# Large on-chip buffers start at multiples of 128 bytes in a decoder layer on one core

## The chip, the cores and the metric

One core of a Trainium2 chip runs the whole layer as one program. Its engines are TensorE (PE in the profile, its weight loads PEld), VectorE (DVE), ScalarE (ACT), GpSimd (POOL) and SyncE (SP), which issues all DMA transfers here. The metric is the device time in microseconds, the median of several executions. The change is about byte addresses within a partition of the on-chip memory (SBUF): every tensor has 128 rows, one for each partition, and starts at the same byte offset in all of them.

## What is computed

A decoder layer over 256 tokens of width 2048, in float32: an input projection, a diagonal state-space branch and a latent attention branch side by side, merged by gates, an output projection with a layer norm, and a gated feed-forward network with a second layer norm.

```python
z = h @ w_in[l]
u_ssm, c_q, c_kv, k_rope_raw, gate_logits = jnp.split(z, split_at, axis=-1)
y_ssm = s5_scan(u_ssm, ...)
glu_a, glu_b = jnp.split(jax.nn.gelu(y_ssm) @ w_glu[l], 2, axis=-1)
ssm_out = glu_a * jax.nn.sigmoid(glu_b)
q = (rms_norm(c_q, q_norm_g[l]) @ w_uq[l]).reshape(bsz, seq, N_HEADS, QK_NOPE + QK_ROPE)
kv = (rms_norm(c_kv, kv_norm_g[l]) @ w_ukv[l]).reshape(bsz, seq, N_HEADS, QK_NOPE + V_HEAD)
mla_out = mla_attention(q_nope, q_rope, k_nope, k_rope, v)
g_ssm, g_mla = jnp.split(jax.nn.sigmoid(gate_logits), 2, axis=-1)
mix = (g_ssm * ssm_out + g_mla * mla_out) @ w_out[l]
h = layer_norm(DEEPNORM_ALPHA * h + mix, ln1_g[l], ln1_b[l])
ffn = (jax.nn.silu(h @ w_ffn_gate[l]) * (h @ w_ffn_up[l])) @ w_ffn_down[l]
h = layer_norm(DEEPNORM_ALPHA * h + ffn, ln2_g[l], ln2_b[l])
```

The feed-forward width is 5632, so its three matrices are most of the weights.

## The kernel before

All weights are packed by the host into 454 slabs of 128 x 1024 float32 (512 KB, 4 KB for each partition) in the order of use. SyncE loads them one after the other into `raw`, a ring of four slots. For each slab ScalarE writes a rounded copy of the type fp32r to `whi` (`high`, L466), and VectorE writes the remainder raw - whi to `wlo` (`low_part`, L421; in the head stage GpSimd takes 16 of them). The activations are split in the same way into a high and a low half, side by side in one buffer. A product of float32 precision is then three fp32r products: high with high, high with low, low with high.

Three helpers on TensorE write these products out:

- `fold_tile` (L823 to L825): stationary operand is a 128 x 128 block of whi or wlo, moving operand 256 columns of the activations. Three matmuls of 256 columns. It runs in the projection stage and for the gates (activations `xT`), in the head stage for the latent projections (`cT`) and in the GLU stage (`yT`).
- `feature_tile` (L834, L837): the same stationary operand; one matmul has the high and the low half, 512 contiguous columns, as its moving operand, and the next has the high half's 256 columns. It runs in the FFN stage (`hT`), 8 pairs in a slab.
- `row_tile` (L845 to L847): the operands are exchanged. The stationary operand is a 128 x 128 block of the activations, the moving operand 512 columns of whi or wlo. It runs for the values (`cT`), the output projection (`mixT`) and the down projection (`act`).

The stages follow each other in the order projection (to about 112 us), four turns of heads with the state-space work (to about 464), GLU (to about 560), output projection (to about 646), first layer norm and turning of h (to about 670), FFN gate and up (to about 1110), down projection (to about 1387), and the second layer norm with the stores.

Where the buffers lie is written by hand in `build`. `at(name, off, shape, dt)` places a tensor at byte `off` of the partition. `raw`, `whi` and `wlo` begin at `base` = 16512 and take 16384 bytes each. Behind them follow seven small tensors of 3104, 192, 192, 32, 32, 32 and 32 bytes (`cst`, `col`, `stats`, `moments`, `rstd`, `sm`, `start`), and the offset behind the last is `a0`. From `a0` on lie `xT`, `rows`, `gb`; from `a1 = a0 + 32768` `cT`, `prod`, `wpad`, `cosT`, `states`, `mixT`, `hT`; from `a2 = a1 + 32768` `kmat`, `tmp`; from `a3 = a2 + 4096` `act` (90112 bytes) and, in the same room at earlier times, `mla`, `xrow`, `gate`, `ustage`, `zT`, `tmpB`, `qT`, `kT`, `u4`, `yb`, `yT`, `ca`, `bbar` and the rest. The lines with a running offset there are:

```python
        xrow = at("xrow", o, [P, 2, D]); o += 16384
        gate = at("gate", o, [P, KT, TOK]); o += 16384
        kT = at("kT", o + 4096, [P, 4, TOK]); o += 10240
        u4 = at("u4", o, [P, PAIRS, NC + 1]); o += PAIRS * (NC + 1) * 4
        wb = at("wb", o, [P, 2, PT, P]); o += 8192
        yT = at("yT", o, [P, UT, 2, TOK], F32R)
```

Of the kernel before, what the change touches and what calls it, by code (L numbers as in the profile page):

```python
# [66 lines left out]

P_CG, P_D, P_G1, P_B1 = 0, 8, 16, 32
P_N = 48

MAGIC = 12582912.0
TWO_PI = 6.283185
# [48 lines left out]
def build(nc, slabs, x, pos, consts, cols, ssm, ssm_b, ssm_c, ln_rows, out):  # L121
    with ExitStack() as ctx:
# [6 lines left out]
        def at(name, off, shape, dt=F32):  # L129
            return nc.alloc_sbuf_tensor_at(name, shape, dt, offset=off)  # L130

        o = base
# [3 lines left out]
        cst = at("cst", o, [P, C_N]); o += 3104  # L136
        col = at("col", o, [P, P_N]); o += 192
        stats = at("stats", o, [P, 2, 4, 6]); o += 192
# [1 line left out]
        rstd = at("rstd", o, [P, 2]); o += 32  # L140
        sm = at("sm", o, [P, 8]); o += 32
        start = at("start", o, [P, 8]); o += 32
        a0 = o

        xT = at("xT", a0, [P, KT, 2, TOK], F32R)
        rows = at("rows", a0, [P, 2, D])
# [19 lines left out]
        o = a3  # L166
# [1696 lines left out]
```

How the kernel before makes its waits and increments, by code:

```python
    def wait(self):  # L109
        self.eng.wait_ge(self.sem, self.base + self.n)
# [144 lines left out]
            def load(at_dram, s, done, count):  # L255
                sy.wait_ge(done, count)
                sy.dma_start(raw[:, s:s + 1, :], slabs[bass.ds(at_dram, 1)].rearrange("a p n -> p a n")
                             ).then_inc(raw_ready[s], 16)
# [1 line left out]
            def skip(s, done, count):  # L261
                sy.wait_ge(done, count)
                sy.sem_inc(raw_ready[s], 16)
# [55 lines left out]
            def spread_u(n):  # L320
                if n == 0:
                    sy.wait_ge(u_zero, 2)
                    for e in range(2):
                        sy.wait_ge(tile_free[e], FREE0[e])
                for b, q in pieces(n):
                    j = (b + 1) % STEP
                    sy.dma_start(u4[32 * b:32 * b + 32, q:PAIRS:4, shift(b):shift(b) + NC],
                                 ustage[32 * q:32 * q + 32, :, j, :]).then_inc(in_u, 16)
# [1 line left out]
            def gather_y(m0, m1, n):  # L331
                if n == 0:
                    sy.wait_ge(bu_psum, HG)
                    sy.wait_ge(y_ready, m1 + 1)
                for b, q in pieces(n):
                    j = (b + 1) % STEP
                    sy.dma_start(yb[32 * q:32 * q + 32, m0:m1, j, :],
                                 u4[32 * b:32 * b + 32, 4 * m0 + q:4 * m1:4, shift(b):shift(b) + NC]).then_inc(in_y, 16)
# [23 lines left out]
            def rows_in(i):  # L363
                sy.wait_ge(slab_used, GLU0)
                sy.dma_start(rows[:, :, bass.ds(i * 512, 512)],
```

## Time and profile before

| | |
|---|---|
| median of 3 runs | 1408.03 us (1408.01 to 1408.79) |
| the profiled execution | 1408.6 us |
| its span, first to last instruction | 1406.1 us |
| TensorE busy, weight loads busy | 1382.0 us (98%), 1244.8 us (89%) |
| VectorE, ScalarE, GpSimd busy | 894.2, 655.2, 61.8 us |
| mean granted TensorE clock | 0.997 |
| moved by DMA | 252.70 MB, 180 GB/s |

The busy time of TensorE is a sum of intervals whose ends are modelled, since matmuls are pipelined. A matmul's record is longer than the distance to the next one's start. For the pace of a stage the distance between starts is the better measure, and the rows below give it from the timeline.

### The profile page before, as it was taken

How to read it: one execution, taken by the hardware profiler on the slowest of the kernel's cores; microseconds unless marked ns; L12 is line 12 of the kernel's file. 1: busy time of each engine (PE TensorE's matmuls, PEld its weight loads, DVE VectorE, ACT ScalarE, POOL GpSimd, SP SyncE). 2: the span in 40 equal slices, each digit the busy share in tenths (PEclk: the TensorE clock that was granted, in tenths of full speed). 3: DMA queues.
4: the chain of work that ended last, by engine and by line, in shares of the span. 5: the costliest groups of instructions: out<-in, count | busy, mean ns of one | idle time of the engine just before them, and what ended most of it. 6: DMA issues, size and time to landing. Idle time of an engine off the chain costs nothing.

```text
span 1406.1 us, 24358 instructions
## 1 busy us (share of the span) xinstructions
PE 1382.0 (98%) x8790; PEld 1244.8 (89%) x8790; DVE 894.2 (64%) x1297; ACT 655.2 (47%) x924; POOL 61.8 (4%) x31
## 2 busy tenths in 40 slices
PE   9999999999999999998999999999999999999996
PEld 8999999999999999886888888888888888888884
DVE  6786766677666666557666666666666654545545
ACT  5557456364464644345444444444444443334332
POOL 1000201202011000000000000000000000000002
PEclk9999999999999999999999999999999999999998
DMA  7566434444354666653655556555555565556562
GB/s 286 180 200 179 146 106 149 134 146 140 117 170 139 213 224 213 205 190 109 209 181 193 192 179 197 191 185 190 191 188 189 189 252 183 190 183 193 168 205 90
DMA packets 80415, 252.70 MB, mean 180 GB/s; under 512 B 17665, under 2 KB 17921, under 8 KB 80257
## 3 DMA queue, kind: packets, MB, share of 16 engines
q1 hardware_dynamic: 80384, 252.31, 54.7%
q8 instruction: 18, 0.29, 0.1%
q14 instruction: 13, 0.10, 0.0%
HBM read 248.08 MB, written 2.10 MB: 178 GB/s over the span
## 4 chain that ended last, share of the span: by engine, by line
PE 93%; DVE 4%; ACT 1%; DMA 1%; issue 1%; SPq 0%; ACTq 0%; DVEq 0%
PE ps L834 22%; PE ps L837 12%; PE ps L823 9%; PE ps L825 9%; PE ps L824 9%; PE ps L845 8%; PE ps L847 8%; PE ps L846 8%; DVE wlo L421 1%; PE ps L966 1%; PE ps L956 1%; PE ps L992 1%; PE ps L993 1%; PE ps L978 1%; PE ps L979 1%
## 5 line engine op out<-in xcount | busy, mean ns | idle before, releaser
L421 DVE TENSOR_TENSOR wlo<-raw,whi 128x1024 fp32r<-128x1024 f32 x438 | 532.0, 1223 | 289.7 <-ACT whi L466 288.9
L466 ACT ACTIVATE whi<-raw 128x1024 fp32r<-128x1024 f32 x454 | 479.1, 1057 | 494.2 <-PE ps L847 191.4
L834 PE MATMUL ps<-hT,whi 128*128 128x512 f32 x1408 | 489.6, 391 | 2.5 <-DVE tmp L1689 1.5
L837 PE MATMUL ps<-hT,wlo 128*128 128x256 f32 x1408 | 397.0, 282 | 0.0
L834 PEld LDWEIGHTS ps<-hT,whi 128*128 128x128 f32 x1408 | 264.2, 188 | 60.3 <-DVE hT L1671 3.1
L837 PEld LDWEIGHTS ps<-hT,wlo 128*128 128x128 f32 x1408 | 266.1, 189 | 0.0
L823 PE MATMUL ps<-xT,whi 128*128 128x256 f32 x784 | 224.8, 287 | 2.0 <-DVE wlo L421 2.0
L824 PE MATMUL ps<-xT,whi 128*128 128x256 f32 x784 | 218.8, 279 | 0.0
L825 PE MATMUL ps<-xT,wlo 128*128 128x256 f32 x784 | 218.7, 279 | 0.0
L823 PEld LDWEIGHTS ps<-xT,whi 128*128 128x128 f32 x784 | 147.5, 188 | 3.4 <-DVE wlo L421 2.2
L824 PEld LDWEIGHTS ps<-xT,whi 128*128 128x128 f32 x784 | 147.5, 188 | 0.4
L825 PEld LDWEIGHTS ps<-xT,wlo 128*128 128x128 f32 x784 | 147.4, 188 | 0.0
L847 PE MATMUL ps<-whi,act 128*128 128x512 f32 x352 | 139.2, 396 | 0.0
L845 PE MATMUL ps<-whi,act 128*128 128x512 f32 x352 | 139.2, 396 | 0.0
L846 PE MATMUL ps<-wlo,act 128*128 128x512 f32 x352 | 139.2, 395 | 0.0
L845 PEld LDWEIGHTS ps<-whi,act 128*128 128x128 f32 x352 | 66.1, 188 | 16.1
L847 PEld LDWEIGHTS ps<-whi,act 128*128 128x128 f32 x352 | 66.1, 188 | 16.0
L846 PEld LDWEIGHTS ps<-wlo,act 128*128 128x128 f32 x352 | 66.1, 188 | 15.9
L823 PE MATMUL ps<-yT,whi 128*128 128x256 f32 x256 | 71.9, 281 | 0.0
L824 PE MATMUL ps<-yT,whi 128*128 128x256 f32 x256 | 71.9, 281 | 0.0
L825 PE MATMUL ps<-yT,wlo 128*128 128x256 f32 x256 | 71.9, 281 | 0.0
L421 POOL TENSOR_TENSOR wlo<-raw,whi 128x1024 fp32r<-128x1024 f32 x16 | 43.8, 2739 | 378.9 <-ACT whi L466 378.9
(243 smaller groups left out, 1535.5 us busy)
## 6 DMA issues: line engine op xcount, KB each, us to landing
raw<-slabs SPq DMA_DIRECT2D x454, 512.0 KB, 3.3
xrow<-x SPq DMA_DIRECT2D x4, 512.0 KB, 6.7
rows<-x SPq DMA_DIRECT2D x4, 512.0 KB, 6.2
gb<-ln_rows SPq DMA_DIRECT2D x4, 512.0 KB, 7.0
gb<-ln_rows SPq DMA_DIRECT2D x1, 2048.0 KB, 7.6
u<-ustage SPq DMA_DIRECT2D x16, 64.0 KB, 3.5
yb<-u SPq DMA_DIRECT2D x16, 48.0 KB, 3.0
out<-rows SPq DMA_DIRECT2D x3, 256.0 KB, 2.5
```

The lines of the kernel that those rows point to most:

```text
L421: unit.tensor_tensor(wlo[:, s, :], raw[:, s, :], whi[:, s, :].bitcast(F32), ALU.subtract).then_inc(done, 1 + empty_after)
L466: nc.scalar.activation(whi[:, s, :], raw[:, s, :], ACT.Copy).then_inc(hi_ready, 1 + empty + first)
L823: mm(ps[:, bank, 0:TOK], hi, src[:, kt, 0, :], start=(first and n == 0), stop=False)
L824: mm(ps[:, bank, 0:TOK], hi, src[:, kt, 1, :], start=False, stop=False)
L825: ins = mm(ps[:, bank, 0:TOK], lo, src[:, kt, 0, :], start=False, stop=(last and n == len(kts) - 1))
L834: mm(ps[:, bank, :], hi, src[:, kt].rearrange("p a t -> p (a t)"), start=(first and n == 0), stop=False)
L837: ins = mm(ps[:, bank, TOK:512], lo, src[:, kt, 0, :], start=False, stop=done)
L845: mm(ps[:, bank, :], xh, hi, start=(first and n == 0), stop=False)
L846: mm(ps[:, bank, :], xh, lo, start=False, stop=False)
L847: ins = mm(ps[:, bank, :], xl, hi, start=False, stop=(last and n == len(kts) - 1))
L956: ins = mm(ps[32 * g:32 * g + 32, YP, (n % 4) * P:(n % 4 + 1) * P], wpad[:, c, n, P - 32:P], ca[:, c, n, :], start=(c == 0), stop=(c == 1))
L966: ins = mm(ps[:, BU + c, n * NC:(n + 1) * NC], wb[:, c, n, :], u4[:, bass.ds(i * PT + n, 1), 0:NC].rearrange("p a k -> p (a k)"), start=Tr ...
```

## The change

One constant is added, and the offset from which the large buffers are placed is rounded up to a multiple of it. No instruction is added, taken away or reordered.

```diff
+LINE = 128
+
...
         start = at("start", o, [P, 8]); o += 32
-        a0 = o
+        a0 = -(-o // LINE) * LINE
 
         xT = at("xT", a0, [P, KT, 2, TOK], F32R)
```

## Rows read from the trace of the kernel before

**Rows 1.** The page: busy time of TensorE, and the ended-last chain by engine.

```profile
PE 1382.0 (98%) x8790; PEld 1244.8 (89%) x8790; DVE 894.2 (64%) x1297; ACT 655.2 (47%) x924; POOL 61.8 (4%) x31
...
PE 93%; DVE 4%; ACT 1%; DMA 1%; issue 1%; SPq 0%; ACTq 0%; DVEq 0%
```

**Rows 2.** Busy time by stretch: opening, FFN, close; columns PE, PEld, DVE, ACT, POOL.

```profile
0.00:30.00 30.00, 27.01 (x194) 24.78 (x194) 17.02 (x38) 17.39 (x27) 3.87 (x8) 1.00 0.83 300
...
670.00:1110.00 440.00, 440.00 (x2540) 390.09 (x2539) 285.05 (x335) 195.72 (x239) 0.00 (x0) 1.00 0.58 190
...
1387.00:1406.10 19.10, 6.13 (x27) 4.60 (x25) 14.58 (x18) 2.65 (x4) 8.69 (x4) 0.77 0.28 110
```

**Rows 3.** TensorE's waits, first and last of eight: us in total, times, longest.

```profile
PE ps L823 <- DVE wlo L421: 2.0, 5, 0.6
...
PE ps L823 <- ACT ustage L491: 0.7, 1, 0.7
```

**Rows 4.** The page's groups of instructions on raw, whi and wlo alone.

```profile
L421 DVE TENSOR_TENSOR wlo<-raw,whi 128x1024 fp32r<-128x1024 f32 x438 | 532.0, 1223 | 289.7 <-ACT whi L466 288.9
L466 ACT ACTIVATE whi<-raw 128x1024 fp32r<-128x1024 f32 x454 | 479.1, 1057 | 494.2 <-PE ps L847 191.4
...
L421 POOL TENSOR_TENSOR wlo<-raw,whi 128x1024 fp32r<-128x1024 f32 x16 | 43.8, 2739 | 378.9 <-ACT whi L466 378.9
```

**Rows 5.** Groups by form on buffers placed from a0 on: VectorE, ScalarE, GpSimd.

```profile
L1671 DVE TENSOR_TENSOR hT<-tmp,hT 128x256 fp32r<-128x256 f32 x16 | 6.4, 419 | 1.9 <-ACT hT L767 1.8
...
L1442 DVE TENSOR_TENSOR prod<-states 128x512 f32<-128x512 f32 x4 | 2.7, 684 | 0.0
...
L574 ACT ACTIVATE yb<-yb 128x1536 f32<-128x1536 f32 x1 | 1.5, 1487 | 0.0
...
L574 ACT ACTIVATE yb<-yb 128x512 f32<-128x512 f32 x1 | 0.6, 622 | 0.0
...
L443 POOL TENSOR_TENSOR rows<-rows,gb 128x1024 f32<-128x1024 f32 x1 | 2.9, 2905 | 953.4 <-ACT rows L795 953.4
```

**Rows 6.** DMA issues of the first 30 us: KB each, median us to landing.

```profile
raw<-slabs SPq DMA_DIRECT2D x10, 512.0 KB, 6.9
...
bpar<-ssm_b SPq DMA_DIRECT2D x1, 512.0 KB, 7.0
```

**Rows 7.** DMA issues of the whole span: the stores of 384 KB.

```profile
out<-rows SPq DMA_DIRECT2D x2, 384.0 KB, 2.5
```

**Rows 8.** Weight loads by form, mean ns: FFN, projection and gates, down, output.

```profile
L834 PEld LDWEIGHTS ps<-hT,whi 128*128 128x128 f32 x1408 | 264.2, 188 | 60.3 <-DVE hT L1671 3.1 <-DVE tmp L1689 1.9
...
L823 PEld LDWEIGHTS ps<-xT,whi 128*128 128x128 f32 x784 | 147.5, 188 | 3.4 <-DVE wlo L421 2.2 <-issue 0.8
...
L845 PEld LDWEIGHTS ps<-whi,act 128*128 128x128 f32 x352 | 66.1, 188 | 16.1
...
L845 PEld LDWEIGHTS ps<-whi,mixT 128*128 128x128 f32 x128 | 24.1, 188 | 5.7
```

**Rows 9.** Timeline of TensorE, down stage (start, length): nine matmuls lie between starts.

```profile
1199.77 0.40 PE L845 MATMUL ps<-whi,act 128*128 128x512 f32 x1
...
1201.87 0.40 PE L845 MATMUL ps<-whi,act 128*128 128x512 f32 x1
```

**Rows 10.** The same, projection stage: 24 matmuls lie between the two starts.

```profile
40.05 0.28 PE L823 MATMUL ps<-xT,whi 128*128 128x256 f32 x1
...
42.85 0.28 PE L823 MATMUL ps<-xT,whi 128*128 128x256 f32 x1
```

**Rows 11.** The same, FFN stage: nine pairs of L834 and L837 lie between.

```profile
699.72 0.39 PE L834 MATMUL ps<-hT,whi 128*128 128x512 f32 x1
...
702.84 0.39 PE L834 MATMUL ps<-hT,whi 128*128 128x512 f32 x1
```

**Rows 12.** The same, GLU stage: 24 matmuls lie between.

```profile
500.06 0.28 PE L823 MATMUL ps<-yT,whi 128*128 128x256 f32 x1
...
502.91 0.28 PE L823 MATMUL ps<-yT,whi 128*128 128x256 f32 x1
```

## The prediction

> **What bounds the kernel now.** I read the page's busy shares and the chain that ended last first. TensorE is busy 1382.0 of 1406.1 us, and the chain is TensorE for 93% and VectorE for 4% [rows 1]. The reader is to see that only what changes TensorE's pace, or the few places where it stands still, can move the time. Next came the stretches by stage: the 440 us of the FFN stage hold 440.00 us of TensorE, the first 30 us hold 27.01, and the 19.10 us after the last full stretch are VectorE's, 14.58 busy [rows 2]. TensorE's own waits add up to 10.6 us, eight entries from 2.0 down to 0.7 us [rows 3]. So the change has three places to act: the time of a matmul or weight load itself, the opening with its loads, and the closing normalisation with its stores.
>
> **What the change moves.** The named small tensors end at byte 69280 of the partition, which is 541 x 128 + 32. The change rounds a0 up to 69376 = 542 x 128. Every buffer that is placed from a0, a1, a2, a3 or the running offset behind a3 moves up by 96 bytes; no instruction, wait, loop or transfer is added or taken away. All steps between these buffers are multiples of 128 (the odd-looking one, u4, is 32 x 65 x 4 = 8320 = 65 x 128), so all of them stood at 32 past a multiple of 128 and now stand on one. raw, whi and wlo start at 16512 = 129 x 128 and were there already. So both kinds of buffer are in the trace of before, and I can price the change by comparing them.
>
> **VectorE.** The costliest group, the low parts (438 of 1223 ns), and ScalarE's high parts (454 of 1057 ns) touch only raw, whi and wlo [rows 4]: nothing changes for them. Are the operations on displaced buffers dearer than these? On VectorE a displaced two-input operation takes 419 ns for 256 elements and 684 ns for 512 [rows 5], that is 265 ns for 256 more; the line through them gives 684 + 2 x 265 = 1214 ns for 1024 elements, and the aligned one takes 1223 ns [rows 4]. The aligned form isn't the cheaper one: between -0.7% and 0. Of the chain VectorE holds 4% [rows 1], some 56 us, so this term is bounded at +0.4 us and I take 0.
>
> **ScalarE and GpSimd.** On ScalarE the displaced yb operations take 622 ns for 512 and 1487 ns for 1536 elements [rows 5]; the value halfway is 1055 ns against 1057 for the aligned 1024. The functions differ, so this is a bound, but a tight one: 0. On GpSimd the aligned 128 x 1024 operation takes 2739 ns, the displaced product of the same size 2905 [rows 4, 5]; there are 16 and 4 such operations, GpSimd's records are rough, and only the last four are near the end, so 6% of 2905 ns, 0.2 us, is the bound and I take 0. All of ScalarE's work in the long stages lies beside a full TensorE anyway.
>
> **DMA.** Slab loads go to aligned raw. In the opening 30 us a 512 KB slab load takes 6.9 us from issue to landing, and 512 KB to displaced bpar, in pieces of the same 4 KB for each partition, 7.0 us [rows 6]: nearly the same. The later loads of rows and gb and the small pieces of u4 and yb land beside a full TensorE, and it waits for none of them [rows 3]. Of the stores only the last counts, 384 KB in 2.5 us [rows 7]. Bounds: 0, and a gain of 0.3 us at either end if some 5% of these transfers were due to the displacement. I take 0. The Trainium skill ("DMA: Bandwidth & Descriptors", How a descriptor splits into AXI transactions) says that a read which doesn't start at a multiple of 256 bytes also fetches the bytes below it. a0 is 160 past such a multiple before and on one after, so an estimate by that page is 5 beats of 32 bytes saved on the 64 of a 2048-byte piece. That would be 8% of the last store, 0.2 us, which no row here confirms and which leaves the forecast as it is.
>
> **TensorE, the term that matters.** Here the displaced buffers are the moving operand of the projection, head, GLU and FFN stages (xT, cT, yT, hT with stationary whi or wlo), and the stationary operand of the v, output and down stages (cT, mixT, act, with moving whi or wlo). A weight load takes 188 ns from whi (1408 and 784 of them) and 188 ns from act or mixT [rows 8]: no difference. A record's own duration is modelled, so I take the distance between starts. Down stage, 512 columns: nine in 2.10 us, 233.3 ns each [rows 9]. Projection, 256 columns: 24 in 2.80 us, 116.7 ns each [rows 10], exactly half of it, one with the moving operand displaced, the other with it aligned. That is the strongest row for no effect. FFN, one of 512 and one of 256: nine pairs in 3.12 us, 346.7 ns [rows 11]; less 116.7 leaves 230.0 for the 512, 3.3 ns less than in the down stage. And GLU, the same code as the projection with yT in place of xT: 24 in 2.85 us, 118.8 ns each [rows 12], 2.1 ns more though yT is as far from a multiple of 128 as xT is (it lies 32 past a multiple of 256 and xT 160). So two small differences in pace exist that the views don't explain, and they are where a placement could matter. I take 0 for the forecast, because the alternation of 512 and 256 columns, or the stage's own order, explains 3.3 ns as well as the address does; the ends are below.
>
> The Trainium skill ("SBUF — State Buffer", Specifications (TRN2)) has lines of 16 bytes, and full bandwidth from two hits in a line on. Starts of 32 and 0 past 128 are both starts of such a line. By that rule no read here takes another line after the change and this term is exactly 0; by the address reading of the rows above it is -5 to +5 us. No run here has shown yet which holds.
>
> Sum: 0 (VectorE) + 0 (ScalarE, GpSimd) + 0 (DMA) + 0 (TensorE). The profiled execution took 1408.6 us for a span of 1406.1; the median of the runs is 1408.03, 0.6 below it. A sum of 0 stands on the median: 1408.0 us.
>
> **Rivals.** *A, displaced weights cost.* The row stages are the ones whose stationary operand is displaced, and their 512-column matmul is 3.3 ns slower than FFN's. If that is the price of the displacement it goes away for 1056 down, 384 output and 96 v matmuls (three times the 352 and 128 of [rows 8], and by the code 32 for each of the three lines in the v tiles): 1536 x 3.3 ns = 5.1 us, 1402.9 us. For it: the difference is steady in both row stages (the two ends of [rows 9] hold over nine matmuls without a gap). Against it: the load itself is 188 ns in both.
>
> *B, the displaced moving operand is the cheap one.* The same 3.3 ns read from the other operand: hT, displaced, streams in 230.0 ns, and whi, aligned, in 233.3. After the change hT is aligned, and 1408 matmuls of 512 columns in the FFN stage take 3.3 ns more: 4.6 us, 1412.6 us. It decides from 2.0 ns each on (2.0 x 1408 = 2.8 us). A variant is GLU's 2.1 ns: were it the price of yT's own residue, and did xT and cT fall into such a one, 784 x 3 = 2352 matmuls with xT [rows 8] and by the code 160 x 3 = 480 with cT would pay it, 2832 in all: 5.9 us, 1413.9 us. For it: two differences that have no other named cause. Against it: 233.3 is twice 116.7 across the two kinds of alignment, and a cost in time for being aligned needs two readers that meet in the same place, which no view shows.
>
> *C, yT alone gains.* If only GLU's 2.1 ns goes, GLU's 768 matmuls (32 slabs of 24) give 1.6 us: 1406.4 us, inside the band of no change.
>
> *D, the change doesn't do what it says.* If some large buffer stayed displaced, or an aligned one was moved off, part of A or B would not show. The arithmetic above excludes it for the buffers placed from a0; the slices inside u4 (260 bytes apart) stay displaced, and their matmuls are 192 of 8790. It gives 1408.0 too.
>
> **How the numbers follow.** A measurement of this kernel tells about 0.2% (2.8 us) from no change. No effect, C and D together: 0.75. A: 0.14. B and its variant: 0.11. Likeliest is 1408.0 us; its own range with the small bounds (0.4 us of VectorE, 0.6 of DMA, 1.6 of C, 0.8 of spread between runs) is 1405.5 to 1409.5. For 8 in 10 it reaches over A and leaves most of B out: 1402.0 to 1411.0.
>
> **What would show it.** Right: in the changed kernel's trace the starts are still 233.3 ns apart in the down stage, 346.7 for the FFN pair, 116.7 in the projection and 118.8 in GLU; TensorE's waits still sum to about 10.6 us, and the stretch after 1387 us stays at 19 us. A is right if the down stage falls to 230.0 and is 3.5 us shorter; B if the pair rises to 350.0; the variant if the projection goes to 118.8; C if GLU goes to 116.7. The DMA bound is wrong if the first slab product starts more than 0.3 us earlier, VectorE's if 419 and 684 ns move by more than 1%. The prediction is wrong if any of these paces moves by 2 ns or more in a stage of over 1400 matmuls.

## The result, and the profile after

The changed kernel takes 1418.31 us (median of 4, 1417.99 to 1418.58), the one before on the same chip 1408.02: a ratio (its time over that of the kernel before) of 1.0072, 95% interval 1.0054 to 1.0089. It is 10.3 us slower. The forecast was no change, 1408.0 us in a range of 1402.0 to 1411.0, so it was wrong.

The new constant adds two lines, so every line number is two higher after. First the page of the changed kernel, where busy time stands by engine and the chain by engine; it answers to [rows 1].

```profile
span 1415.6 us, 24358 instructions
...
PE 1392.9 (98%) x8790; PEld 1252.4 (88%) x8790; DVE 895.3 (63%) x1297; ACT 654.8 (46%) x924; POOL 61.2 (4%) x31
...
PE 94%; DVE 4%; ACT 1%; issue 0%; DMA 0%; SPq 0%; ACTq 0%; DVEq 0%
```

The number of instructions is the same on every engine. The span is 9.5 us longer, and TensorE is busy for 10.9 us more. VectorE (+1.1), ScalarE (-0.4) and GpSimd (-0.6) don't account for it. Next the stretches between the first matmuls of the stages, cut at the same events in both kernels: projection with heads, GLU, output, FFN, down. First the kernel before, then the changed one. The columns are those of [rows 2].

```profile
11.90:465.50 453.60, 451.19 (x3692) 440.27 (x3693) 320.66 (x624) 248.29 (x433) 49.26 (x19) 1.00 0.49 158
465.50:556.70 91.20, 91.20 (x771) 91.20 (x770) 62.70 (x96) 44.77 (x66) 0.00 (x0) 1.00 0.69 231
556.70:646.00 89.30, 89.30 (x385) 71.97 (x384) 50.49 (x55) 35.92 (x37) 0.00 (x0) 1.00 0.56 182
653.60:1146.60 493.00, 490.46 (x2820) 432.70 (x2819) 321.13 (x387) 222.80 (x283) 0.00 (x0) 1.00 0.58 192
1146.60:1392.70 246.10, 246.10 (x1057) 198.15 (x1056) 118.15 (x110) 93.55 (x90) 1.26 (x1) 1.00 0.54 176
```

```profile
11.60:469.20 457.60, 456.00 (x3692) 445.31 (x3693) 320.96 (x624) 248.17 (x433) 48.63 (x19) 1.00 0.48 156
469.20:561.40 92.20, 92.20 (x771) 92.20 (x770) 62.49 (x96) 44.59 (x66) 0.00 (x0) 1.00 0.71 228
561.40:650.40 89.00, 89.00 (x386) 72.16 (x385) 50.50 (x55) 35.94 (x37) 0.00 (x0) 1.00 0.55 182
658.00:1157.10 499.10, 496.57 (x2819) 433.23 (x2818) 322.32 (x387) 222.58 (x283) 0.00 (x0) 1.00 0.56 190
1157.10:1402.20 245.10, 245.10 (x1057) 198.74 (x1056) 118.05 (x110) 93.60 (x90) 1.26 (x1) 1.00 0.54 176
```

The reader is to take the differences of the lengths: +4.0, +1.0, -0.3, +6.1 and -1.0 us. With the opening (-0.3), the first layer norm (7.6 us in both) and the close (13.4 us in both) that is the whole +9.5. TensorE is all but full in these stretches in both kernels, at a granted clock of 1.00, and its waits over the whole span fell from 10.6 to 9.0 us. So it isn't waiting more, it is going slower. Where activations are the moving operand the stage is longer, where they are the stationary one it is a little shorter. The same is to be seen in the distance between starts in the changed kernel, which answers to [rows 10] to [rows 12] and [rows 9]: projection (24 matmuls), GLU (24), FFN (nine pairs), down (nine).

```profile
40.14 0.28 PE L825 MATMUL ps<-xT,whi 128*128 128x256 f32 x1
...
42.99 0.28 PE L825 MATMUL ps<-xT,whi 128*128 128x256 f32 x1
...
500.19 0.28 PE L825 MATMUL ps<-yT,whi 128*128 128x256 f32 x1
...
503.07 0.28 PE L825 MATMUL ps<-yT,whi 128*128 128x256 f32 x1
...
699.92 0.40 PE L836 MATMUL ps<-hT,whi 128*128 128x512 f32 x1
...
703.08 0.40 PE L836 MATMUL ps<-hT,whi 128*128 128x512 f32 x1
...
1199.59 0.39 PE L847 MATMUL ps<-whi,act 128*128 128x512 f32 x1
...
1201.68 0.39 PE L847 MATMUL ps<-whi,act 128*128 128x512 f32 x1
```

Groups of three in the projection now take 2.85 us / 8 = 356 ns (350.0 before), in GLU 2.88 / 8 = 360 (356), FFN's pair 3.16 / 9 = 351.1 (346.7), and three in the down stage 3 x 2.09 / 9 = 697 (700). 1408 pairs x 4.4 ns = 6.2 us is FFN's whole loss, and 352 x 3 ns = 1.1 us is what the down stage gains.

### The profile page after: what moved, and what is told of

It reads as the page before. It is cut to its first block, busy times and chain, and to the rows that moved or that the text cites. A ratio compares the mean times of both kernels' runs of the same rounds, so it can differ in the third digit from the quotient of the medians.

```text
span 1415.6 us, 24358 instructions
## 1 busy us (share of the span) xinstructions
PE 1392.9 (98%) x8790; PEld 1252.4 (88%) x8790; DVE 895.3 (63%) x1297; ACT 654.8 (46%) x924; POOL 61.2 (4%) x31
## 4 chain that ended last, share of the span: by engine, by line
PE 94%; DVE 4%; ACT 1%; issue 0%; DMA 0%; SPq 0%; ACTq 0%; DVEq 0%
PE ps L836 22%; PE ps L839 12%; PE ps L825 10%; PE ps L827 9%; PE ps L826 9%; PE ps L849 8%; PE ps L847 8%; PE ps L848 8%; PE ps L968 1%; PE ps L958 1%; DVE wlo L423 1%; PE ps L994 1%; PE ps L995 1%; PE ps L980 1%; PE ps L981 1%
## 5 line engine op out<-in xcount | busy, mean ns | idle before, releaser
L836 PE MATMUL ps<-hT,whi 128*128 128x512 f32 x1408 | 495.7, 394 | 2.5 <-DVE tmp L1691 1.5
L1691 DVE TENSOR_REDUCE tmp<-ps 128x256 f32<-128x512 f32 x88 | 60.5, 687 | 1.4
```

Of the source, the lines that this page charges most:

```text
L836: mm(ps[:, bank, :], hi, src[:, kt].rearrange("p a t -> p (a t)"), start=(first and n == 0), stop=False)
L1691: V.tensor_reduce(out_, ps[:, bank, :].rearrange("p (a t) -> p t a", a=2), mybir.AxisListType.X, ALU.add).then_inc(row_free, 1)
```

## The experiments

The theories. *Theory 1*: TensorE's pace depends on where its two operands lie, and it gets in its own way; the kernel's other engines have no part in it. *Theory 2*: accesses of other engines or of DMA collide with TensorE's reads at certain addresses. *A plain rule of 128*: a start at a multiple of 128 bytes is dear by itself.

### A kernel of TensorE alone

Only the three patterns of the helpers are left, in sections with other addresses: fold (`fold_tile`, three matmuls of 256 columns), feat (`feature_tile`, one of 512 and one of 256) and row (`row_tile`, three of 512). w stands for whi (and 16384 bytes on, wlo), x for the activations. Each section is one line, so that its first start can be read from the timeline. The list of sections is written short here.

```python
SECTIONS = [(k, r, 128) for k in ("fold", "feat", "row") for r in range(0, 512, 32)] + ...
ws = {rw: wfull[:, rw // 4:rw // 4 + 5120] ...}     # weights rw bytes past a multiple of 512
xs = {rx: xfull[:, rx // 4:rx // 4 + 4096] ...}     # activations rx bytes past one
for n, f, l, c0, c1, w_, m_ in seq('fold', 64, 128): ins = mm(ps[:, 0, c0:c1], w_, m_, start=f, stop=l)
for n, f, l, c0, c1, w_, m_ in seq('fold', 96, 128): ins = mm(ps[:, 0, c0:c1], w_, m_, start=f, stop=l)
```

> A kernel of TensorE work alone: all layers' work is left out, the output is a copy of one result block. It repeats the pattern of each helper (fold: three of 256 columns; feat: 512 and 256; row: three of 512) in sections of 24 repeats, each with its activation buffer at another distance from a multiple of 512 bytes, and with whi and wlo at 128 past one as in the layer; all other engines and the DMA queues are idle. Theory 1, TensorE is slowed by its own two reads (weights and moving columns) at certain addresses: the paces of the layer come back, fold 350 ns for three at 160 (xT before), 356 at 32 (yT before), 357 at 0 (xT after), 360 at 128 (yT after); feat 346.7 for two at 160 and 351 at 0; row 700 for three at 160 and 697 at 0. Theory 2, other engines' or the DMA's accesses to the memory collide with TensorE's reads: every section of one pattern has the same pace within 0.3%. Then further sections move the weights' address, and one repeats a single matmul.

The page of this kernel, and then the starts of four sections (L204 has x at 64, L205 at 96, L206 at 128, L207 at 160, all with w at 128; 24 groups of three in each).

```profile
PE 882.2 (97%) x5952; PEld 814.3 (90%) x5952; ACT 10.7 (1%) x5; POOL 0.2 (0%) x4
...
37.54 0.63 PE L204 MATMUL ps<-xfull,wfull 128*128 128x256 f32 x4
...
45.72 0.51 PE L205 MATMUL ps<-xfull,wfull 128*128 128x256 f32 x3
...
54.23 0.64 PE L206 MATMUL ps<-xfull,wfull 128*128 128x256 f32 x4
...
62.86 0.40 PE L207 MATMUL ps<-xfull,wfull 128*128 128x256 f32 x2
```

While TensorE runs there is no work on any other engine. Still, (45.72 - 37.54) / 24 = 340.8 ns for three at 64, (54.23 - 45.72) / 24 = 354.6 at 96, and (62.86 - 54.23) / 24 = 359.6 at 128. This is the same code with the same number of columns, and it differs by 5.5%. Theory 2 foretold one pace for all sections of a pattern and falls as the explanation. Two paces of the layer didn't come back where they were expected: at 160 fold took 353.8 ns (expected 350) and at 32 it took 352.1 (expected 356). Both expected values came up at these places in the second kernel below. The sections named `one` in the kernel repeat one weight block and one block of 256 columns 72 times, and three such matmuls take what fold takes at the same eight places of x, within 0.4 ns (340.8 at 64, 355.0 at 96, 359.6 at 128). So neither the walk from block to block nor the turn from whi to wlo makes the difference.

The sections that move w as well as x order themselves by one number, the distance d = (place of w - place of x) modulo 256. Four pairs of places for each (ns for three, fold):

```
d      x=0           x=32          x=128         x=160
  0    w=0   359.6   w=32  359.6   w=128 359.6   w=160 359.6
 32    w=32  355.0   w=64  354.6   w=160 355.0   w=192 354.6
 64    w=64  353.3   w=96  353.8   w=192 340.8   w=224 353.3
 96    w=96  352.1   w=128 352.1   w=224 360.0   w=0   352.1
128    w=128 355.8*  w=160 355.8   w=0   356.2   w=32  355.8
160    w=160 360.0   w=192 359.6   w=32  360.0   w=64  359.6
192    w=192 353.3   w=224 353.3   w=64  353.3   w=96  353.3
224    w=224 353.8   w=0   350.0   w=96  353.3   w=128 353.7
* read at x=256; the section at 0 was the first, before TensorE was at its pace
```

Five rows hold within 0.4 ns. The rows 64, 96 and 224 each have one entry or more that stands out, so distance isn't all: there is a second pace for some distances. Nor is it a matter of the residues alone: with w at 128, x at 64 took 340.8 ns and x at 320, the same place modulo 256, took 353.3 (L212, 105.45 to 113.93 us), both behind a fold section at 32 modulo 256. Only fold was measured with w moved; for feat and row the place of w was 128 throughout in this kernel.

### The layer with other places for all buffers, and for all but one

```diff
-        a0 = o
+        a0 = o + 32      # f_p32;  o + 64 in f_p64
```

> The whole layer, with a0 at 69312: all large buffers move up by 32 instead of 96 bytes (xT, cT, hT, mixT, act at 192 past a multiple of 256, yT at 64). If only a start at a multiple of 128 is dear, as the diff's own rule turned round would have it, 1408 us. If the pace goes by the distance between the buffers and whi and wlo (theory 1), it differs from 1408 by several us either way, and FFN's pair is not 346.7 ns.

> The same with a0 at 69344, 64 bytes up (xT, cT, hT, mixT, act at 224 past a multiple of 256, yT at 96). If only multiples of 128 are dear: 1408 us. By theory 1 it stands where the quiet kernel's sections for these places say, by stage.

1416.23 us (ratio 1.0058, 1.0041 to 1.0075) and 1421.22 us (1.0092, 1.0075 to 1.0109). No large buffer stands at a multiple of 128 in the first, and the long ones don't in the second, which is the slowest of all. The plain rule of 128 falls, in its own direction and turned round. Over groups of 32 starts the paces are those of the quiet kernel for the same places: in f_p64 the projection takes 360.0 ns for three (359.6 there), FFN's pair 350.0 (350.4) and the down stage 702.8 (702.5). In f_p32 FFN's pair takes 353.3 (352.1), but the projection 340.0 where the quiet kernel had 353.3. The profile of f_p32 is of its shortest run, 1413.81 us; the other three took 1415.96 to 1416.54. In that profile the projection begins at 353 ns for three, as in the quiet kernel, and changes at a wait for VectorE's low part (these are the starts of the first line of each three):

```profile
28.70 0.28 PE L823 MATMUL ps<-xT,whi 128*128 128x256 f32 x1
29.05 0.28 PE L823 MATMUL ps<-xT,whi 128*128 128x256 f32 x1
29.79 0.38 PE L823 MATMUL ps<-xT,whi 128*128 128x256 f32 x1 [0.23 <-DVE wlo L421]
30.24 0.28 PE L823 MATMUL ps<-xT,whi 128*128 128x256 f32 x1
30.58 0.28 PE L823 MATMUL ps<-xT,whi 128*128 128x256 f32 x1
```

So a row of the table that held within 0.4 ns (192) isn't proof of a single pace either.

```diff
-        a1 = a0 + 32768
+        a1 = a0 + 32768 + 96     # a0 stays as before
```

> The changed layout, but xT, rows and gb stay where they were (a1 and all behind it move up by 96). Where each buffer's own place sets the pace, the matmuls with xT (2352 of the 2832 that cost 4.0 us in the stages before GLU) return to 116.7 ns and the rest keeps the changed kernel's pace: 1418.3 - 3.3 = 1415.0 us. Where the layout as a whole or something else decides, 1418 us.

1414.98 us (ratio 1.0049, 1.0032 to 1.0066), 3.3 below the changed kernel, as worked out. With xT left in its place, the time between the first matmuls of projection and GLU is 454.8 us (11.4 to 466.2), near the 453.6 of before, while GLU, output and FFN keep the changed kernel's lengths within 0.1 us. The pace expected for xT didn't come back: the projection takes 353.3 ns for three (117.8 each), not 350.0. f_row128 below shows 353.3 as well, with xT at the same place, and the profiles of the kernel before and of f_allup 350.0. So the agreement of the total to 0.1 us is in part luck. Each buffer's own place counts, stage by stage.

### Everything moved together

```diff
-        base = 16512
+        base = 16512 + 96        # a0 not rounded
```

> The whole layer with base itself 96 bytes up, so every buffer, raw, whi and wlo too, moves up by 96 bytes and a0 is not rounded. xT, cT, hT, mixT and act stand exactly where the changed kernel has them, at multiples of 256; only their distance to whi and wlo is that of before. Theory 1 by distance: 1408.2 us within 0.8, FFN's pair 346.7 ns, GLU 356 for three. Absolute place of the large buffers decides: 1418.3 us, pair 351.

1408.14 us, ratio 0.9999 (0.9989 to 1.0009). The timeline of FFN in this kernel, nine pairs between the two starts:

```profile
699.12 0.39 PE L834 MATMUL ps<-hT,whi 128*128 128x512 f32 x1
...
702.24 0.39 PE L834 MATMUL ps<-hT,whi 128*128 128x512 f32 x1
```

3.12 us / 9 = 346.7 ns, as in [rows 11], with hT at the very byte at which the changed kernel needs 351.1. So the loss doesn't come from where the large buffers start. It comes from their having moved by 96 bytes against whi and wlo, which stayed. This is also the one run in which w has another place than 128 under the patterns feat and row.

### One buffer repaired, and the paces foretold

```diff
-        hT = at("hT", a1, [P, KT, 2, TOK], F32R)
+        hT = at("hT", a1 + 32, [P, KT, 2, TOK], F32R)
-        a2 = a1 + 32768
+        a2 = a1 + 32768 + 32     # on the changed kernel
```

> The changed kernel, but hT 32 bytes further on (32 past a multiple of 256) and with it all from a2 on: no buffer of FFN, GLU or down stands at a multiple of 128 any more, xT, cT and mixT still do. By the quiet kernel's table of distances: FFN's pair 351.1 to 347.1 ns (1408 pairs, -5.6 us), yT at 160 for 128 past (360.0 to 350.0 for three, 256 groups, -2.6 us), act at 32 for 0 (697 to 700.4, 352 groups, +1.2 us): 1418.3 - 7.0 = 1411.3 us. If FFN's loss had another cause than hT's place, 1415 us or more.

1411.21 us (median of 10, ratio 1.0019, 1.0009 to 1.0028): 0.1 us from the sum. The starts in FFN:

```profile
699.81 0.39 PE L836 MATMUL ps<-hT,whi 128*128 128x512 f32 x1
...
702.93 0.39 PE L836 MATMUL ps<-hT,whi 128*128 128x512 f32 x1
```

Again 3.12 us for nine pairs, 346.7 ns. The largest part of the loss goes with hT's place. tmp and act moved along with it, but TensorE reads neither in this stage.

### Towards a layout that is faster

In the quiet kernel's row pattern the pace at d = 0 is 680.4 ns for three against 700 at the place of before. f_row128 puts mixT and act there.

```diff
-        mixT = at("mixT", a1, [P, KT, 2, TOK], F32R)
+        mixT = at("mixT", a1 + 224, [P, KT, 2, TOK], F32R)
-        a3 = a2 + 4096
+        a3 = a2 + 4096 + 224
-        theta = at("theta", a3 + FT * 2 * TOK * 4, [P, PAIRS])
+        theta = at("theta", a2 + 4096, [P, PAIRS])
```

> The kernel before, with mixT and act (and all else from a3 on) 224 bytes up, so that both stand like whi and wlo at 128 past a multiple of 256; theta moves into the gap ahead of a3, xT, cT and hT stay. Theory 1 by distance: row_tile falls from 700.0 to 680.4 ns for three (d = 0), 480 groups of three x 19.6 = 9.4 us less, GLU's yT comes to d = 128, 355.8 instead of 356.2: 1408.2 - 9.4 = 1398.8 us. Were the quiet kernel's pace not reachable beside the other engines: 1408 us.

1399.23 us, ratio 0.9935 (0.9919 to 0.9952). The down stage of this kernel, three matmuls between neighbouring starts of one line (two of these distances are left out):

```profile
1198.65 0.39 PE L845 MATMUL ps<-whi,act 128*128 128x512 f32 x1
...
1200.69 0.39 PE L845 MATMUL ps<-whi,act 128*128 128x512 f32 x1
...
1201.37 0.39 PE L845 MATMUL ps<-whi,act 128*128 128x512 f32 x1
```

(1201.37 - 1198.65) / 4 = 680 ns for three, where [rows 9] give 700. Here mixT and act are 128 bytes past a multiple of 256, like whi.

f_best also brings the fold stages to d = 64, where the quiet kernel had its fastest fold; f_row128y64 does so for yT alone. The edit is shortened, the old line of theta goes.

```diff
+        theta = at("theta", o, [P, PAIRS])
-        a0 = o
+        a0 = o + 160             # xT and cT at 64
-        mixT = at("mixT", a1, ...)         hT the same
+        mixT = at("mixT", a1 + 64, ...)    # mixT, hT, act at 128
-        a2 = a1 + 32768
+        a2 = a1 + 32768 + 64
-        wb = at("wb", o, [P, 2, PT, P]); o += 8192
+        wb = at("wb", o, [P, 2, PT, P]); o += 8192 + 64     # yT at 64; this line alone on top of f_row128 in f_row128y64
```

> All operands of the long products at the places where the quiet kernel was fastest: xT, cT and yT at 64 past a multiple of 256 (d = 64), hT, mixT and act at 128 (d = 0), theta in the gap ahead of a0. row_tile 680.4 ns for three (-9.4 us), FFN's pair 346.7 as before. fold_tile at d = 64 has had two paces: if it takes the fast one, 340.8 ns for three, 944 groups x 9.2 + 256 x 15 ns = 12.6 us less, 1386 us; if the slow one, 353.3, 3.1 us more in the stages before GLU and 0.7 less in GLU, 1401 us.

> f_row128 with yT and what lies behind it 64 bytes further on (64 past a multiple of 256, d = 64 for GLU), xT, cT and hT still as before. GLU's three matmuls go to 340 ns, as in f_best, 256 groups x 15.7 = 4.0 us: 1399.2 - 4.0 = 1395.2 us, and the runs agree within 1 us, since FFN stays at d = 224. If f_best's wide spread comes from yT's place, this kernel spreads by several us too.

> f_best once more, unchanged, to see which stage its spread of 8.5 us comes from. The quiet kernels had two paces for feat at 128 past, 346.7 and 353.0 ns, 6.3 x 1408 = 8.9 us. If the FFN stage flips between them from one execution to the next, the runs lie at or between 1390.5 and 1399.4 us, and a profile with a time near the upper end shows the pair at 353 ns and 499 to 501 us between the first matmuls of FFN and of down instead of 493; one with GLU or the head stage longer would put the flip there.

f_best has a median of 1393.45 us (ratio 0.9907, 0.9882 to 0.9932), but its four runs lie at 1390.6, 1391.5, 1395.4 and 1399.1, and again six lie between 1390.5 and 1401.8 (median 1396.3, ratio 0.9916, 0.9887 to 0.9946). Neither comes down to the 1386 us of the fast case: in the first profile (the run of 1390.6) the row stages are 9.4 us shorter, as reckoned, and GLU 4.1, where 3.8 was, but the 944 groups before GLU bring 4.1 us (453.6 to 449.5) and not 8.7. f_row128y64 takes 1395.25 us, as worked out (ratio 0.9913, 0.9897 to 0.9930), with three runs at 1395.1 to 1395.4 and one at 1398.2, so they don't all agree within 1 us. So my expectation for the place of the spread, FFN, found no support: in both profiles of f_best the pair is 346.7 ns. The profile of the second, a run of 1393.28 us, shows a flip in GLU. These are the starts of the first line of each three, with the one weight load that waited:

```profile
487.26 0.28 PE L823 MATMUL ps<-yT,whi 128*128 128x256 f32 x1
487.60 0.28 PE L823 MATMUL ps<-yT,whi 128*128 128x256 f32 x1
487.94 0.28 PE L823 MATMUL ps<-yT,whi 128*128 128x256 f32 x1
488.43 0.19 PEld L823 LDWEIGHTS ps<-yT,whi 128*128 128x128 f32 x1 [0.19 <-DVE wlo L421]
488.43 0.38 PE L823 MATMUL ps<-yT,whi 128*128 128x256 f32 x1
488.89 0.28 PE L823 MATMUL ps<-yT,whi 128*128 128x256 f32 x1
489.24 0.28 PE L823 MATMUL ps<-yT,whi 128*128 128x256 f32 x1
489.60 0.28 PE L823 MATMUL ps<-yT,whi 128*128 128x256 f32 x1
```

340 ns for three up to 487.94, one wait of 0.19 us for VectorE's low part, and 350 to 360 (353.3 over groups of 32 further on) for the rest of the stage. Nothing but that wait lies between, as in f_p32 above, where the pace changed the other way. Other waits leave the pace as it was: the projection of f_best in its first profile stands still after 28.5 us and after 67.9 us and runs at 340 ns for three before and behind both. So a wait is where the pace can change; what decides it isn't shown. The stage takes 89.6 us instead of 87.0 in the first profile of f_best. A GLU that is slow from its start costs 256 x 13.3 ns = 3.4 us, and f_row128y64's one odd run is 3.0 above its others. xT and cT stand at the same distance: 944 x 13.3 = 12.6 us at most, more than the spread of f_best. No profile shows one of f_best's runs above 1399 us, so that their excess lies in those stages is an inference, and which stage spreads stays open.

### What sets the second pace

The quiet kernel in steps of 16 bytes, then with other predecessors, and a third with longer sections (40 groups).

> TensorE alone again, all else left out, in steps of 16 bytes (and at 4 and 8) of the activation buffer with whi and wlo at 128 past a multiple of 256, in falling order; then six sections again, each behind four different predecessors. Theory 1 with the distance d = (weights - activations) modulo 256 as the only variable: the values at steps of 32 come back whatever the order (fold 359.6 at d = 0 and 160, 355.8 at 128, 353.3 at 192; row 680.4 at 0, 687.1 at 64, 700 at 224, feat 347.1 at 96 and 224). Theory 1b, the pace also locks to what ran before: fold at d = 64 comes out as 340.8 behind one predecessor and 353.3 behind another. Theory 3, lines of 16 bytes count by themselves: 4 and 8 are 15 ns or more above 0 and 16, and steps of 16 are as good as steps of 32.

> TensorE alone, all else left out: fold at eight places, 40 groups each, behind three different predecessors (feat, row, and a full float32 matmul of 128 columns), and feat and row at six places behind two. If distance alone sets the pace, each place has one value whatever ran before. If the pace also locks to the order of what ran before, fold at d = 64, 96, 160 and 224 changes by 3 to 20 ns for three between predecessors and keeps its value through 40 groups, and feat and row change less.

The third kernel, fold with x at 64 and w at 128: L208 behind feat, L224 behind row, with the start of what follows each.

```profile
48.20 0.28 PE L208 MATMUL ps<-xfull,wfull 128*128 128x256 f32 x1
...
62.33 0.39 PE L209 MATMUL ps<-xfull,wfull 128*128 128x512 f32 x1
...
287.25 0.40 PE L224 MATMUL ps<-xfull,wfull 128*128 128x256 f32 x2
...
300.86 0.39 PE L225 MATMUL ps<-wfull,xfull 128*128 128x512 f32 x1
```

14.13 us / 40 = 353.2 ns behind feat and 13.61 / 40 = 340.3 behind row. Addresses, code and idle engines are the same; the predecessor differs. The second kernel gave the same two values behind the same two patterns (353.3 and 340.4), so it is hardly chance. But the predecessor isn't all: the two sections at 64 and 320 above followed like predecessors and differed. Over the three quiet kernels, with w at 128 (ns for a group, the first section of each left out, and those behind the full float32 matmul, which hold some 0.1 us of the switch from it):

```
x      d      fold            feat            row
  0    128    355.8 - 360.2   350.8 - 351.4   697.0 - 700.0
 32     96    352.1 - 360.0   347.1           700.0 - 700.4
 64     64    340.3 - 353.3   352.5 - 353.3   686.8 - 687.5
 96     32    354.6 - 355.0   352.5 - 353.3   699.6
128      0    359.5 - 360.0   346.7 - 353.3   680.0 - 681.7
160    224    350.0 - 360.0   346.5 - 347.5   699.6 - 700.4
192    192    353.2 - 353.3   348.8 - 353.3   700.0 - 700.7
224    160    359.2 - 360.0   350.0 - 350.4   702.5
```

Fold has two or three paces at some places (350, 353 and 360 at x = 160; 352, 356 and 360 at x = 32), feat two at some, and row two at x = 0: 697 in most sections, 700 behind the folds at 32, 96 and 224 and once behind the fold at 160. Row at d = 0 kept one pace in all of its sections. So the values of the first kernel didn't come back whatever the order (in the second, fold at x = 32 took 355.8 for 352.1 and feat at x = 128 took 346.7 for 353.3), and the expectation that the pace locks to what ran before was the better one. In the third kernel it held for fold at d = 64 (13 ns between predecessors), at 96 (360.0 behind feat, 356.0 behind row) and at 224 (350 behind both, 353.4 in the second half of the section behind the full float32 matmul), not at 160. Feat and row changed less, by up to 6.6 and 3 ns. In steps of 16 the values between don't follow their neighbours (fold takes 341.7 ns at 240, 360.0 at 224 and 208, 357.5 at 80 and at 48), so "steps of 16 are as good" in the expectation was wrong as far as it meant an even curve. At 8 and 4 bytes past a multiple of 16 fold takes 366.2 and 372.1 and feat 360.4 and 355.0, against 355.8 and 350.8 at 0; the 15 ns or more of the expectation are reached by fold at 4 alone. The Trainium skill ("SBUF — State Buffer", Specifications (TRN2)) has lines of 16 bytes with a price for each new line; these two fold and feat sections agree with it. Row doesn't (699.6 and 682.5, against 697.5 at 0), and there it is the stationary operand that is off.

## Why the prediction was wrong

**The small terms held.** VectorE's two forms take 420 and 684 ns after (419 and 684 in [rows 5]), ScalarE's 621 and 1488 (622 and 1487), GpSimd's 2909 (2905), the stores of 384 KB 2.5 us as in [rows 7], bpar's load 6.8 us (7.0 in [rows 6]) beside slabs that went from 6.9 to 6.5. The last store has 3072 bytes for each partition (columns 768 to 1536), not the 2048 of the estimate of 0.2 us, and stores of both sizes take 2.5 us before and after. The opening is 0.3 us shorter, at the bound given for it, but that says little: its length is 11.4 to 12.3 us over the profiles of the layer. The close is the same. That part of the sum was 0 and measured 0 to -0.3.

**The step that failed is TensorE's term, taken as 0.** It measured +9.8 us (+4.0 +1.0 -0.3 +6.1 -1.0). Three sentences of it went wrong.

First, the comparison of classes. I priced the change by comparing displaced buffers with aligned ones, each with its own residue to 128. A matmul has two operands, and what counts is how far they lie from each other, modulo 256 bytes, with a second pace at some distances: d went from 224 to 128 for xT, cT and hT, and from 96 to 0 for yT. "Both kinds of buffer are in the trace" was true and didn't help, since the distances that the change makes, d = 128 and for yT d = 0, aren't among those of the long stages before.

Second, "the strongest row for no effect": 233.3 ns in the down stage is twice 116.7 in the projection [rows 9, 10]. Both stages happened to stand at d = 224, where the two patterns give 700 and 350. The quiet kernel has 680 and 360 at d = 0. The equality was one point of two curves.

Third, the two small differences that I did find and set aside. FFN's 3.3 ns per matmul of 512 columns was put down to the alternation of widths. That can stand: at the old distance (d = 224) the quiet kernels also have 346.5 to 347.5 for feat beside 350.0 for fold and 700 for row, so no difference of address is needed for it, though width and the exchange of roles weren't tried apart. But GLU's 2.1 ns, with the same code as the projection, could only be its place or the order ahead of it. That one row said that a placement can cost 1.8% somewhere, and it deserved more than a variant inside a rival of 0.11.

**The rivals.** The sign of B was right for the moving side, and its prices were near: 4.6 us in FFN against 6.1 measured, and 5.9 for xT and cT against 4.0 in a stretch that also has attention and waits in it. Its reason was wrong in saying that a displaced operand is cheap in itself; f_allup shows that it isn't. It gave 0.11 of the chance. It also held the argument that would have carried it: "two readers that meet in the same place, which no view shows". The quiet kernels leave TensorE's own two reads as the only readers of SBUF. A had the right stages and price for a different place: aligned weights gave 1.3 us here, but the row stages have 9.4 us in them when d is 0 (f_row128). C went the other way: yT lost 1.0 us. D was right on the arithmetic of the addresses.

**The rule that I leaned on.** By the lines of 16 bytes the term was "exactly 0". The runs show that this rule isn't the only thing: all places from 0 to 224 in steps of 32 are multiples of 16, and fold runs from 340 to 360 ns. The Trainium skill ("TensorE: Matmul & The Clock Gate", Step-by-step: what each phase is for) also says that TensorE has two independent read ports and that loading the next weights takes no read bandwidth from the running matmul. The measurements decide against that for fp32r operands as they are here: a pace that goes with the distance between weights and columns, with all other engines idle, says that the two affect each other. How they do it is an inference that no run shows.

**What stays open.** Which of the reads meet (the load for the next matmul with the running one's columns, or others), and why in 256 bytes, was not tried apart. Nor is it known what in the order of events picks one of the paces. That the same section keeps either of two behind two predecessors is shown twice; that a wait can change the pace in mid-stage is seen in two profiles, each once.

## What to carry to other kernels

Where TensorE sets the time, the places of its two operands relative to each other were worth up to 5% of a stage here (GLU: 87.0 us at d = 64, 92.2 at d = 0), and rounding one side to a tidy multiple while the other stays can cost as much as it can bring. Measure the pace of each pattern in a kernel of TensorE alone over the distances to 256 bytes, place the buffers by that table, and prefer a distance with a single pace (here row at d = 0) to a faster one with two. And when a stage with the same code and shapes runs at another pace than its sister, take that as a price of something the change may touch, not as a curiosity.

## What the runs showed that was not expected

- A group of three fp32r matmuls of 256 columns takes 340.3 to 360.2 ns, one of three with 512 columns 680.0 to 702.5, by where its operands lie, with every other engine idle and all starts at multiples of 32 bytes. The distance modulo 256 bytes orders them, most clearly where a place has one pace.
- Moving every buffer by 96 bytes changes nothing (1408.14 against 1408.31 us), moving all but the weights costs 10.3 us.
- The same section of the same kernel at the same addresses runs at 340.3 or 353.2 ns for three behind two different predecessors, keeps its pace through 40 groups, and in the layer one wait of 0.19 us within GLU changed it for the rest of the stage. Kernels with a fold stage at d = 64 spread by 3 to 11 us from run to run, where the kernel before spreads by 0.6 to 1.5.
- A layout alone, with the same 24358 instructions, takes 1395.25 us with a spread of 3.1 (f_row128y64), or 1390.5 to 1401.8 (f_best), against 1408.3 before.
